# Mixture-of-experts layer on one core: dense gates placed by adding indirect DMAs instead of one-hot products, and the low parts of the keys made on VectorE

## The reference, cut to what matters

```python
s = jnp.einsum('thzd,hzkd->thzk', qry, sub_keys)
top_s, top_i = lax.top_k(s, 16)
cand_s = (top_s[:, :, 0, :, None] + top_s[:, :, 1, None, :]).reshape(nt, 8, 256)
cand_i = (top_i[:, :, 0, :, None] * 128 + top_i[:, :, 1, None, :]).reshape(nt, 8, 256)
best_s, best_pos = lax.top_k(cand_s, 16)
idx = jnp.take_along_axis(cand_i, best_pos, axis=-1)
gate = jax.nn.softmax(best_s, axis=-1)
act = gelu(jnp.einsum('td,thkd->thk', tb, expert_u[ib]))
out = jnp.einsum('thk,thkd->td', act * gate, expert_v[ib])
```

## Time and profile before

| | us |
|---|---|
| median of 3 runs | 2761.29 (2757.78 to 2764.63) |
| the profiled execution | 2742.67 |
| its span, first to last instruction | 2740.9 |
| the matmuls of up_stage, first to last | 1217.6 to 2081.9 |
| busy in the span: PE / DVE / POOL / ACT | 91% / 61% / 53% / 35% |

### The profile page before, as it was taken

How to read it: one execution, slowest core, us unless ns; L and a number is a source line. 1 busy time by engine, 2 the same in 40 slices (tenths; PEclk the granted TensorE clock), 3 DMA queues, 4 the chain that set the end, 5 groups by cost and what they waited for, 6 DMA issues and landing times. The chain is left out here.

```text
span 2740.9 us, 35437 instructions
## 1 busy us (share of the span) xinstructions
PE 2495.9 (91%) x11629; PEld 2025.9 (74%) x11629; DVE 1658.4 (61%) x2562; ACT 959.5 (35%) x1340; POOL 1463.7 (53%) x893
## 2 busy tenths in 40 slices
PE   7998887888699997989899999999997999999977
PEld 5886476777678886877787777778775788887765
DVE  4333566777642122145798489389404999999842
ACT  5444212333333222313452443354233333333322
POOL 3442254666543342424664574475446888888841
PEclk9999767899899998999999999999998999999989
DMA  3220000000022221314338336434765999999930
GB/s 143 92 92 31 1 0 6 1 0 0 31 94 91 93 92 59 110 39 138 100 103 243 115 98 208 149 102 146 237 216 201 344 350 346 345 347 336 332 133 31
DMA packets 175499, 383.26 MB, mean 140 GB/s; under 512 B 18128, under 2 KB 100176, under 8 KB 167632
## 3 DMA queue, kind: packets, MB, share of 16 engines
q1 hardware_dynamic: 152912, 315.32, 34.0%
q0 software_dynamic: 22528, 67.19, 7.3%
HBM read 321.63 MB, written 60.82 MB: 140 GB/s over the span
## 5 line engine op out<-in xcount | busy, mean ns | idle before, releaser
L1400 POOL TENSOR_TENSOR up_u_low_sb<-up_u_sb,up_u_high_sb 128x1024 fp32r<-128x1024 f32 x128 | 328.9, 2570 | 415.9 <-ACT up_u_high_sb L1505 415.9
L173 PE MATMUL ps<-n_high_sb,up_u_high_sb 128*128 128x512 f32 x1024 | 413.5, 404 | 23.0 <-POOL up_u_low_sb L1400 22.8
L174 PE MATMUL ps<-n_low_sb,up_u_high_sb 128*128 128x512 f32 x1024 | 407.1, 398 | 0.0
L175 PE MATMUL ps<-n_high_sb,up_u_low_sb 128*128 128x512 f32 x1024 | 407.1, 398 | 0.0
L1754 PE MATMUL ps<-down_v_high_sb,down_w_high_sb 128*128 128x512 f32 x768 | 302.7, 394 | 28.7 <-POOL down_v_low_sb L1677 28.5
L1755 PE MATMUL ps<-down_v_low_sb,down_w_high_sb 128*128 128x512 f32 x768 | 300.0, 391 | 0.0
L1756 PE MATMUL ps<-down_v_high_sb,down_w_low_sb 128*128 128x512 f32 x768 | 299.9, 391 | 0.0
L173 PEld LDWEIGHTS ps<-n_high_sb,up_u_high_sb 128*128 128x128 f32 x1024 | 195.1, 191 | 77.0 <-POOL up_u_low_sb L1400 34.6
L1651 ACT ACTIVATE down_v_high_sb<-down_v_sb 128x1024 fp32r<-128x1024 f32 x128 | 125.0, 1048 | 351.1 <-PE ps L1756 337.0
L1006 POOL TENSOR_TENSOR merge_low_sb<-merge_slots_sb,merge_high_sb 128x2048 fp32r<-128x2048 f32 x28 | 129.3, 4620 | 221.2 <-ACT merge_high_sb L1000 221.2
L175 PEld LDWEIGHTS ps<-n_high_sb,up_u_low_sb 128*128 128x128 f32 x1024 | 194.6, 190 | 46.1
(11 more groups left out here) (315 smaller groups left out, 5657.2 us busy)
## 6 DMA issues: line engine op xcount, KB each, us to landing
up_u_sb<-expert_u SPq DMA_DIRECT2D x128, 512.0 KB
down_v_sb<-expert_v SPq DMA_DIRECT2D x128, 512.0 KB
a_dense<-up_gelu_sb SPq DMA_DIRECT2D x128, 256.0 KB
g_dense<-up_gates_sb SPq DMA_DIRECT2D x24, 1024.0 KB
down_gelu_sb<-a_dense SPq DMA_DIRECT2D x128, 192.0 KB
down_gates_sb<-g_dense SPq DMA_DIRECT2D x128, 192.0 KB
w_slots_sb<-w_conv SPq DMA_DIRECT2D x20, 1024.0 KB, 4.8
merge_slots_sb<-w_gates SPq DMA_DIRECT2D x16, 1024.0 KB
```

The source lines that it names most:

```text
L173: pe.matmul(out, ah, bh, start=k == 0, stop=False)
L174: pe.matmul(out, ah, bl, start=False, stop=False)
L175: last = pe.matmul(out, al, bh, start=False, stop=k == n - 1)
L1400: pool.tensor_tensor(ul[:, n, :, :], u[:, n, :, :], bits32(uh[:, n, :, :]), ALU.subtract).then_inc(low, 1)
```

## The change

- The dense gates are no longer made by products. DVE computes for each chosen expert the address of its cell in `g_dense` (`place`), and POOL issues an indirect DMA for each of the 128 choices of a tile that adds one gate for each of 128 tokens to its cell: 384 DMAs of 128 single elements. After every 16 (one head), POOL waits until all that it has issued for this tile have landed.
- The cells must be zero before. `g_dense` is filled with zeros in `gdn_stage`, two stages ahead of `query_stage`: 8 DMAs of SP from a zero tile, 3.1 MB each.
- The turning of the keys, the one-hot rows, POOL's products, ACT's copies and SP's stores of the gates go. So do the loops of ACT, SP and POOL: they are written out. PE keeps a loop, of four keys.
- `u_low` moves from POOL to DVE. DVE makes two of them at the start and then one whenever `spent` has counted 4.2 us of its own choosing work (the costs are written into the calls); those that are left follow in a row.
- The rings of `u`, `u_high`, `u_low` and `gelu` have four slots instead of two.
- Of down_stage's first loads, `v` is loaded during keys 100 to 107; gelu and gates are loaded after the last key is stored and all gates have been added. down_stage is otherwise the same.

```diff
@@ gdn_stage
+    nought = work.take("nought", [P, TD])
+            sp.wait_ge(nought_made, 1)
+            for j in range(0, PEER_K, CLEAR):
+                sp.dma_start(m.g_dense[j:j + CLEAR].rearrange("j i t -> i j t"),
+                             nought[:, :].unsqueeze(1).broadcast_to([P, CLEAR, TD])).then_inc(cleared, 16)
+            sp.wait_ge(cleared, 16 * (PEER_K // CLEAR))
...
+            pool.memset(nought[:, :], 0.0).then_inc(nought_made, 1)
@@ up_stage, vector
+            def low_part():
+                j, n = split[0], split[0] % RING
+                dve.wait_ge(high, j + 1)
+                dve.tensor_tensor(ul[:, n, :, :], u[:, n, :, :], bits32(uh[:, n, :, :]), ALU.subtract).then_inc(low, 1)
+                split[0] += 1
+            def spent(us):
+                split[1] += us
+                if split[1] >= PACE and split[0] < PEER_K:
+                    split[1] -= PACE
+                    low_part()
...
-                    last = top16(scores[:, hz, :], spare[:, hz * PEER_K:(hz + 1) * PEER_K], top_v[:, hz, :], top_i[:, hz, :])
+                    last = top16(scores[:, hz, :], spare[:, hz * PEER_K:(hz + 1) * PEER_K], top_v[:, hz, :], top_i[:, hz, :], 1.7)
...
+                st.done(dve.scalar_tensor_tensor(at_f[:, :], second, float(P), first, ALU.mult, ALU.add))
+                st.done(dve.scalar_tensor_tensor(at_f[:, :], at_f[:, :], float(TD if tt < DENSE else T),
+                                                 token[:, tt:tt + 1].broadcast_to([P, HK]), ALU.mult, ALU.add))
+                if tt < DENSE:
+                    dve.tensor_copy(place[:, tt, :], at_f[:, :]).then_inc(placed, 1)
...
-                with dve.Fori(0, P // STEP) as i:
-                    for b in range(FOURS):
...
-                        dve.tensor_tensor(hot_h[:, four, :], iotas, spread_over(high_t[:, 1, t]), ALU.is_equal).then_inc(second_eq, 1)
-                        dve.tensor_tensor(hot_i[:, four, :], iotas, spread_over(high_t[:, 0, t]), ALU.is_equal)
-                        dve.wait_ge(second_eq, k)
-                        dve.tensor_tensor(hot_l[:, four, :], bits32(hot_h[:, four, :]), spread_over(gate_l[:, t]), ALU.mult).then_inc(second_low, 1)
@@ up_stage, sync
+            for j in range(PEER_K):
+                if j + RING < PEER_K:
+                    sp.wait_ge(low, j + 1)
+                    load(j + RING)
+                sp.wait_ge(gelu, j + RING + 1)
+                sp.dma_start(a_dense[j], av[:, j % RING, :]).then_inc(a_stored[j % RING], 16)
+                if j in range(PREFETCH_AT, PREFETCH_AT + 2 * DOWN_J):
+                    b, n = divmod(j - PREFETCH_AT, DOWN_J)
+                    down.load_v(sp, b, b, n)
+            for tt in range(DENSE):
+                sp.wait_ge(added[tt], 16 * HK)
+            for n in range(RING):
+                sp.wait_ge(a_stored[n], 16 * (BLOCKS + 1))
+            for b in range(2):
+                for j in range(DOWN_J):
+                    down.load_weights(sp, b, b, j)
@@ up_stage, gpsimd
+            for tt in range(DENSE):
+                pool.wait_ge(placed, tt + 1)
+                for h in range(PEER_H):
+                    if h:
+                        pool.wait_ge(added[tt], 16 * TOPK * h)
+                    for k in range(h * TOPK, (h + 1) * TOPK):
+                        at = bass.IndirectOffsetOnAxis(ap=place[:, tt, k:k + 1], axis=0)
+                        pool.indirect_dma_start(cells, at, gates[:, tt, k:k + 1], None, compute_op=ALU.add).then_inc(added[tt], 16)
@@ up_stage, tensor
+            with pe.Fori(0, BLOCKS) as i:
+                for n in range(RING):
+                    pe.wait_ge(low, i * RING + (n + 1))
+                    pe.wait_ge(gelu, i * RING + (n + 1))
+                    products(pe, m.ps[:, n, :], [(uh[:, n, k, :], ul[:, n, k, :]) for k in range(KT)],
+                             [(m.nh[:, k, :], m.nl[:, k, :]) for k in range(KT)]).then_inc(prod, 1)
```

More of the change, by code:

```diff
@@ L1327, in up_stage @@
     best, pos, part = take("best", [P, PEER_H, TOPK]), take("pos", [P, PEER_H, TOPK], U32), take("part", [P, HK], U32)
[L1328 to L1335, removed]
@@ L1336, in up_stage @@
-    sem = lambda name: m.sem(f"up_{name}")
[L1337 to L1341, removed]
+    part_f, sums, token = take("part_f", [P, HK]), take("sums", [P, PEER_H]), take("token", [P, TT])
@@ L1342, in up_stage @@
+    chosen, at_f = take("chosen", [P, 2, HK]), take("place", [P, HK])
+    gates, place = take("gates", [P, DENSE, HK]), take("gate_at", [P, DENSE, HK], U32)
+    sem = lambda name: m.sem(f"up_{name}")
+    dve_s, exped, placed, maxed = (sem(x) for x in ("dve_steps", "gate_exp", "gates_placed", "best_less_max"))
+    added = [sem(f"gates_added{tt}") for tt in range(DENSE)]
+    u_in, a_stored = [sem(f"u{n}_loaded") for n in range(RING)], [sem(f"gelu{n}_stored") for n in range(RING)]
     high, low, prod, gelu = sem("u_high_done"), sem("u_low_done"), sem("products"), sem("gelu_done")
@@ new lines, in _, with load @@
+                spent(2.0)
+            for n in range(split[0], PEER_K):
+                low_part()
+        @block.sync
+        def _(sp):
+            def load(j):
+                sp.dma_start(u[:, j % RING, :, :].rearrange("p k i -> p (k i)"), eu[j]).then_inc(u_in[j % RING], 16)
+            for n in range(RING):
+                sp.sem_inc(a_stored[n], 16)
+                load(n)
+            for j in range(PEER_K):
[14 more added lines that the diff above has]
+                    down.load_weights(sp, b, b, j)
@@ L1498, in _, with split @@
         @block.scalar
         def _(act):
-            act.sem_inc(gs_done, FOURS)
-            act.sem_inc(gelu, 2)
-            def split(j, n):
-                act.wait_ge(u_in[n], j * 8 + (16 - 8 * n))
+            act.sem_inc(gelu, RING)
+            def split(j):
+                n = j % RING
+                act.wait_ge(u_in[n], 16 * (j // RING + 1))
                 act.activation(uh[:, n, :, :], u[:, n, :, :], ACT.Copy).then_inc(high, 1)
-            def key(j, n, more=True):
+            for n in range(RING):
+                split(n)
@@ L1509, in key @@
+            for j in range(PEER_K):
+                for tt in range(TT):
+                    if j == max(exp_at[tt] - RING + 1, 0):
+                        gate = gates[:, tt, :] if tt < DENSE else m.v_gate[:, tt - DENSE, :]
+                        act.wait_ge(maxed, tt + 1)
+                        act.activation(gate, gate, ACT.Exp).then_inc(exped, 1)
+                n = j % RING
                 act.wait_ge(prod, j + 1)
-                act.wait_ge(a_stored[n], j * 8 + (16 - 8 * n))
+                act.wait_ge(a_stored[n], 16 * (j // RING + 1))
@@ L1538, in _ @@
[L1538 to L1548 removed]
+                if j + RING < PEER_K:
+                    split(j + RING)
```

214 lines of the change are left out of this document (42 added, 172 removed).

## The result

The changed kernel takes 3071.46 us (3066.97 to 3076.89), the kernel before 2759.53 us in the same comparison: ratio 1.1135, interval 1.1098 to 1.1171. It is 11% slower where the prediction said 2627 us. The profiled execution took 3066.97 us, its span is 3065.2.

A forecast was written before the change was run, and what follows sets the result against it. PE was taken to bound up_stage, busy 824.8 of 864.3 us. Keys -143 and moved issues +9 gave -134: 2742.7 to 2608.7, or 2627 us as median, being 18.6 higher; range 2604 to 2745, the forecast's own 2603 to 2640.

The forecast's parts named there:

- change 2: up_stage, POOL: 384 adding DMAs at 1.51 us each, done at 714 us, hidden behind PE by 17 us.
- p = 1.90: up_stage, POOL: issue and pause per add, in us, from which the loss eats the 134 us won.
- p = 2.68: up_stage, POOL: us per add if descriptors cost twice the gather's, 2.38 + 0.30; POOL 432 us late, 3059 us.
- rival 2: up_stage, POOL's issue: adds are dear and the kernel gets slower, priced at 3059 us; chance 0.14.
- Change 1: up_stage: PE does only keys, 128 at 5.63 us, 721 us in place of 864.3; 143 us won.
- Waits for landing: up_stage, POOL: after every 16 adds a wait of 1.5 us, 24 of them, 36 us.
- the sum: POOL's end in up_stage, 98 + 384 x 1.51 + 24 x 1.5 = 714 us; for the whole kernel, -143 + 9 = -134.
- Change 3: End of up_stage: sixteen issues for gelu and gates between last store and barrier, 8.8 us lost.
- Change 4: gdn_stage: writing 25.2 MB of zeros takes 77 us at 325 GB/s and costs nothing.
- the slack: up_stage: POOL's adds done 17 us before the stage's end, more if later issues cost the shorter 1.25 us.
- the first rival: up_stage: the adds end the stage but cost less than they win, 2640 to 2752 us; chance 0.20.

The follow-up runs named there:

- `e2_one_tile`: Changed kernel with the gates of only the first tile added, 128 adding DMAs in place of 384: 2613.56 us, ratio 0.9481.

## Why the prediction was wrong, point by point

- **The step that failed** is in change 2: the price of an add, taken from the gather's issue and pause as 1.51 us. An add costs 2.70 us without the heads' waits (1079.5 of 384 issues and pauses less 44, by the group's row and the first and last start). The issue is 1.63, in place of the 1.22 mean of the gathers: 156 us. The pauses are 1.07 in place of 0.29: 301 us. The gather of single elements was the nearest row, but an add's issue and its pauses are its own. The prediction counted 128 descriptors for such a gather; no run shows its descriptors, and the packets of queue 0 are 144 for an add and 32 for a plain write of as many elements. The issue alone eats the gain: 384 adds at 1.93 us (1.63 and the gather's 0.30) with 88 us ahead and 44 of waits end at 873 us of the stage, some 150 behind PE, and the other terms had won 134; the pauses alone cost more.
- **The deciding comparison** was known: p = 1.90 was the point from which the change loses, and p = 2.68 gave 3059 us. The rival was given 0.14 with no row against it but one of another operation. The bounds came from a gather's shortest and longest rows, which bound a gather. That rival 2 comes within 12 us of the measured time is luck in its parts: it doubled an issue and left the pause at 0.30, where the issue grew by a third and the pause nearly fourfold; its 2.68 us and the measured 2.70 agree only in sum.
- **Change 1** was right in kind and size: -145 us in `e2_one_tile`, -148 in the changed kernel, where I had -143. Keys took 5.58 us for 5.63; DVE kept up (PE waited 7.7 us for the first low part, before the first key, and never again), a low part took 1.22 us.
- **Waits for landing** at the heads: 44 us for 36. There are 21 of them (POOL doesn't wait at a tile's first head), 2.1 us each, where the sum had 24 of 1.5. The first add came 88 us after DVE's first instruction of the stage (1212.76), not 98: the sum had paced the first tile by PE's keys, 91 us, but DVE set it. From its first low part, at 1217.64, to the first add it took 83 us, of which about 1 was waiting; the sum had DVE's own work at 83.6.
- **Change 3**: 7.6 us for 8.8 where PE sets the end.
- **Change 4**: nothing, as said. gdn_stage's window has the same PE time (225.6 and 224.4 us) with the DMAs at 0.27 in place of 0.01.
- **Issues and pauses beside the keys**: all that the adds' issues took over the shortest, 1.54 us, is 624.3 - 384 x 1.54 = 33 us. They took 1.71, 1.61 and 1.55 us in the mean in the three tiles, of which the third lies behind the keys. The pauses and the heads' waits, too, are longer while the keys run: the pauses last 2.55, 2.35 and 1.91 us in the mean. Against the third tile that is 61 us, and no run tells whether DVE or the weights' loads stretch them; that an issue is shorter where DVE works less was my estimate in the slack and in the first rival. Both together are 94 us of the 446 that SP waits, so this can be a part, not the cause.
- **The rest of the sum**: with the adds hidden the change gave 2613.56 - 2753.85 = -140 us against the kernel before in the same comparison, where the sum said -134.

## What to carry to other kernels

An operation that the trace doesn't hold has no price from its nearest relative: where its count is in the hundreds and the break-even is 1.3 times the relative's price, the chance of a loss is large, and the point from which the change loses deserves more weight than the slack. Count an indirect DMA's issue for each instruction, not for each partition (half the partitions saved 0.14 of 1.55 us), and look whether pauses come at fixed numbers: then `dynamic_dma_scratch_size` may set them, and is a cheap thing to try (2870.39 us with 2048, 3071.46 with 1024). And sums that an idle engine can make ahead (336 short instructions of DVE at 0.23 us) were cheaper than letting the DMA add (2637.22 us for 2870.39, both with 2048).

## What the runs showed of the hardware that was not expected

- The issue of an indirect DMA over 128 partitions: 0.96 us for a write of single elements, 1.55 for an add; 1.41 for an add over 64 partitions.
- Long pauses of POOL (1.7 to 5.4 us) at fixed numbers of DMAs by scratch size (before the adds that are multiples of 3 and 7 with 1024, of 7 with 2048), even with one DMA in flight; a pause lasts as long as a wait for landing (1.93 and 1.94 us at 512, behind the keys); from 512 to 2048 the cost of an add falls from 4.04 to 2.34 us, and the whole kernel's time from 3737.63 to 2870.39.
- The same kernel's down_stage took 541.4 and 551.1 us in two profiles: a single profile bounds no term under 10 us there.
